# A new front for a hybrid mLSTM / Fourier layer: position products before the modulation, and both modulation halves on TensorE

## What is computed

```python
mod = silu(c) @ w_mod + b_mod
sh1, sc1, g1, sh2, sc2, g2 = split(mod, 6)
h = x * (1 + sc1) + sh1
proj = h @ w_in                       # q, k, v, o, gates, uf, ga, gb
y_b = fourier(uf) @ w_branch_b        # DFT over positions and over the channels of a group
merged = sigmoid(ga) * y_a + sigmoid(gb) * y_b      # y_a: bidirectional mLSTM
x = layer_norm(ALPHA * x + g1 * (merged @ w_out))   # then a SwiGLU FFN, modulated by sh2, sc2, g2
```

## Time and profile before

| | us |
|---|---|
| median of 3 runs (lowest, highest) | 1384.87 (1383.64, 1385.35) |
| span of the profiled execution, first to last instruction | 1382.7 |
| PE busy | 1361.7 |
| VectorE, POOL, ScalarE busy | 860.4, 747.3, 467.1 |
| granted TensorE clock, mean | 0.999 of full |

### The profile page before, as it was taken

How to read it: one execution, slowest core, us unless ns; L and a number is a source line. 1 busy time by engine, 2 the same in 40 slices (tenths; PEclk the granted TensorE clock), 3 DMA queues, 4 the chain that set the end, 5 groups by cost and what they waited for, 6 DMA issues and landing times.

```text
span 1382.7 us, 23138 instructions
## 1 busy us (share of the span) xinstructions
PE 1361.7 (98%) x8693; PEld 1294.0 (94%) x8693; DVE 860.4 (62%) x1458; ACT 467.1 (34%) x828; POOL 747.3 (54%) x417
## 2 busy tenths in 40 slices
PE   9999999999999999999999999989999999999997
PEld 5999999899899989999999999988999999988886
DVE  6875984357426724753587376487877777764307
ACT  4834321231222122221324100266554455463220
POOL 0274775632462354145335666455988889852440
PEclk9999999999999999999999999999999999999999
DMA  9633643211412231142027555613222212242321
GB/s 382 226 108 137 214 149 133 79 64 55 142 68 67 94 109 46 65 145 76 30 91 237 190 183 187 170 64 137 92 91 91 91 62 89 92 168 76 122 77 76
DMA packets 59563, 165.07 MB, mean 119 GB/s; under 512 B 8152, under 2 KB 22624, under 8 KB 58216
## 3 DMA queue, kind: packets, MB, share of 16 engines
q1 hardware_dynamic: 38712, 143.53, 30.3%
q10 hardware_dynamic: 20784, 20.69, 4.7%
HBM read 146.86 MB, written 17.34 MB: 119 GB/s over the span
## 4 chain that ended last, share of the span: by engine, by line
PE 67%; DVE 11%; issue 8%; POOL 6%; DMA 4%; ACT 3%; SPq 0%; DVEq 0%; ACTq 0%; POOLq 0%
PE psum L1425 19%; PE psum L998 15%; PE psum L1462 11%; PE psum L1315 8%; PE psum L1297 3%; PE psum L1063 3%; POOL w_hi L820 3%; POOL w_lo L824 2%; DVE nt_a L2406 2%; PE psum L1169 2%; PE psum L1253 2%; DMA raw<-in_wunits 2%; PE psum L1055 1%; DVE yl L2448 1%; PE psum L1027 1%
## 5 line engine op out<-in xcount | busy, mean ns | idle before, releaser
L820 POOL TENSOR_TENSOR w_hi<-raw,zero 128x1024 fp32r<-128x1024 f32 x78 | 152.3, 1952 | 346.7 <-PE psum L998 280.9
L824 POOL TENSOR_TENSOR w_lo<-raw,w_hi 128x1024 fp32r<-128x1024 f32 (+1 forms) x111 | 268.8, 2422 | 130.6 <-ACT w_hi L2111 73.5
L1425 PE MATMUL psum<-t_r,ws_r 128*128 128x322 f32 x1848 | 276.6, 311 | 2.0 <-POOL ws_r L898 0.7
L1425 PEld LDWEIGHTS psum<-t_r,ws_r 128*128 128x128 f32 x1848 | 275.0, 189 | 3.2 <-issue 2.0
L998 PE MATMUL psum<-h_hi,w_hi 128*128 128x256 f32 (+1 forms) x768 | 176.2, 310 | 1.1 <-PEq L1361 1.0
L998 PE MATMUL psum<-h_lo,w_hi 128*128 128x256 f32 (+1 forms) x768 | 174.9, 309 | 0.0
L998 PE MATMUL psum<-h_hi,w_lo 128*128 128x256 f32 (+1 forms) x768 | 174.8, 309 | 0.0
L898 POOL TENSOR_TENSOR ws_r<-ws_f,ws_r 128x512 fp32r<-128x512 f32 x88 | 124.1, 1410 | 33.7 <-DVE ws_f L2675 20.9
L998 PEld LDWEIGHTS psum<-h_hi,w_hi 128*128 128x128 f32 x768 | 137.8, 188 | 2.4 <-issue 1.7
L998 PEld LDWEIGHTS psum<-h_lo,w_hi 128*128 128x128 f32 x768 | 139.8, 188 | 0.0
L998 PEld LDWEIGHTS psum<-h_hi,w_lo 128*128 128x128 f32 x768 | 139.7, 188 | 0.0
(11 more groups left out here) (359 smaller groups left out, 3070.3 us busy)
## 6 DMA issues: line engine op xcount, KB each, us to landing
raw<-in_wunits SPq DMA_DIRECT2D x124, 512.0 KB, 3.4
pair<-in_wunits SPq DMA_DIRECT2D x46, 512.0 KB, 4.3
mod_slot<-in_wmod SPq DMA_DIRECT2D x16, 512.0 KB, 14.5
mod_ring<-in_wmod ACTq DMA_DIRECT2D x16, 512.0 KB, 3.5
yg_dram<-yg_sb ACTq DMA_DIRECT2D x20, 256.0 KB, 3.0
yg_st<-yg_dram SPq DMA_DIRECT2D x16, 320.0 KB, 3.8
c_raw<-in_stateC SPq DMA_DIRECT2D x4, 1028.0 KB, 6.6
z_ring<-in_wmod SPq DMA_DIRECT2D x8, 512.0 KB, 4.4
```

Of the source, the lines that this page charges most:

```text
L820: pool.tensor_tensor(hi, src, zero[:, 0:1].broadcast_to([P, src.shape[1]]), ALU.add)\
L824: pool.tensor_tensor(lo, src, hi.bitcast(F32), ALU.subtract).then_inc(w_split, 1)
L1425: ins = mm(out, ws_r[n][:, w, cols], t_r[:, n, k, x, :], start=(starts and k == 0 and m == 0), stop=(k == HALF_K - 1 and m == 2), skip_gro ...
```

## The change

- PE's queue: 28 idle products; then all eight odd position tiles, fold by fold over eight banks; the first four scale tiles, three even position tiles, four scale tiles, three even tiles, the transposes, two even tiles; the odd sides of weight 0; all eight shift tiles (first 0, 1, 2, 6, then 7, 3, 4, 5) as two-row products; the odd sides of weight 1 with the shift's transposes after three blocks; the even sides. A modulation part takes the tiles in turn for the first 512 columns, then for the second.
- ScalarE copies position tiles out unscaled in one piece (position_out) and applies the scale when it rounds (position_round, two pieces). VectorE's rest is a two-piece product with a subtraction (e_rest). The zero-position columns go through fix_f, with a rest of their own.
- VectorE loses the sixteen sums of shift_tile, the even sums and the rests of weights 0 and 1; POOL gets the latter two. The bias is added by VectorE (mod_columns).
- SP loads the odd half of the table, the folds, the even half, bmod, eight scale tiles, two weights and five shift tiles; the other three shift tiles follow when the scale parts are done. The table of x, the c rows and weights 2 and 3 follow when the shift parts are done. ScalarE's SiLU of the c rows moves from 22 us to behind h_round(7), ahead of gw_hi.

The diff, cut to its core:

```diff
-POS_BANKS = (4, 5, 6, 7, 2, 3)
+POS_BANKS = (*range(8), 2, 3, 4, 5, 6, 7, 2, 3)
+ROWS_AT = (0, 6)
...
-        N_IDLE = 44
+        N_IDLE = 28
...
-            sp.dma_start(d_st[:], dft_pos).then_inc(table_in, 16)
-            sp.dma_start(bmod_sb[:], bmod).then_inc(bmod_in, 16)
+            sp.dma_start(d_st[:, 1, :, :], dft_pos[:, 1, :, :]).then_inc(table_in, 16)
             for i in range(KT):
                 sp.dma_start(x_rep[:, i, :], x_fold[0, i]).then_inc(xf_in[i], 16)
                 sp.dma_start(x_par[:, i, :], x_fold[1, i]).then_inc(xf_in[i], 16)
...
+            sp.dma_start(d_st[:, 0, :, :], dft_pos[:, 0, :, :]).then_inc(x_in[2], 16)
+            sp.dma_start(bmod_sb[:], bmod).then_inc(bmod_in, 16)
+            scale_in(*range(KD))
             weights(0)
             weights(1)
...
+            for k in (0, 1, 2, 6):
+                shift_in(k)
+            sp.wait_ge(c_sb_in, 16)
+            shift_in(7)
+            sp.wait_ge(mod_done, 2)
+            for k in range(3, 6):
+                sp.wait_ge(shift_landed[k].sem, shift_landed[k].base)
+                shift_in(k)
+            for n in range(3):
                 x_part(n)
...
+            sp.wait_ge(mod_done, 5)
             sp.dma_start(dx_st[:], dft_x).then_inc(table_in, 16)
+            sp.dma_start(silu_z[:], c_rows).then_inc(row_in, 16)
...
+            pool.memset(c_pad[:], 0.0).then_inc(zero_ok, 1)
+            for i in range(KT):
+                pool.wait_ge(fold_ok, i + 1)
+                pool.tensor_tensor(x_rep[:, i, :], x_rep[:, i, :], x_par[:, i, :], ALU.add).then_inc(fold_even_ok, 1)
+            for u in range(2):
+                src, hi, lo = split(u, u, True, n_in=16)
+                pool.wait_ge(w_half, u + 1)
+                rest(src, hi, lo)
...
-            def scale_part(n):
-                pe.wait_ge(mod_in[n], 16)
+            def mod_part(kind, ks, first, last):
+                for k in ks:
+                    if kind == 0:
+                        pe.wait_ge(mod_in[k], 16)
+                    else:
+                        pe.wait_ge(shift_landed[k].sem, shift_landed[k].base + 16)
                 for half in range(2):
-                    ins = mm(psum[0:2, half, :], c_silu[:, n, :], slots[n][:, half * 512:(half + 1) * 512],
-                             start=(n == 0), stop=(n == KD - 1))
+                    for n, k in enumerate(ks):
+                        tile = slots[k if kind == 0 else S_HOME[k]]
+                        ins = mm(psum[0:2, ROWS_AT[kind] + half, :], c_pad[:, k, :],
+                                 tile[:, half * 512:(half + 1) * 512], start=first and n == 0,
+                                 stop=last and n == len(ks) - 1)
                 ins.then_inc(mod_done, 1)
...
+                span = slice(NRC if t else 0, NR)
+                for n, (x, d) in enumerate(((hi, d_hi), (lo, d_hi), (hi, d_lo))):
+                    ins = mm(psum[:, POS_BANKS[i], span], x[:, t, cols], d[:, kind, t, span],
+                             start=(t == 0 and n == 0), stop=(t == KT - 1 and n == 2), skip_group_check=True)
+                return ins
+            def odd_positions():
+                pe.wait_ge(table_ok, 1)
                 for t in range(KT):
...
+                    pe.wait_ge(fold_lo_ok, t + 1)
+                    for i in range(KD):
+                        ins = position_rows(i, t)
+                        if t == KT - 1:
+                            ins.then_inc(pos_done, 1)
+            def even_position(i):
+                if i == KD:
+                    pe.wait_ge(table_ok, 2)
+                    pe.wait_ge(fold_lo_ok, 2 * KT)
+                pe.wait_ge(pos_free, i - 5)
+                for t in range(KT):
+                    ins = position_rows(i, t)
                 ins.then_inc(pos_done, 1)
...
-            for n in range(2):
-                scale_part(n)
-            for i in range(2):
-                position(i)
-            for n in range(2, 6):
-                scale_part(n)
-            position(2)
-            for n in range(6, KD):
-                scale_part(n)
-            position(3)
-            scale_columns()
-            for i in range(4, 2 * KD):
-                position(i)
+            odd_positions()
+            pe.wait_ge(pos_free, 2)
+            mod_part(0, range(4), True, False)
+            for i in range(KD, KD + 3):
+                even_position(i)
+            mod_part(0, range(4, KD), False, True)
+            for i in range(KD + 3, KD + 6):
+                even_position(i)
+            mod_columns(0)
+            for i in range(KD + 6, 2 * KD):
+                even_position(i)
             pe.wait_ge(mod_ready, 1)
-            pe.wait_ge(pos_free, 12)
...
+            pe.wait_ge(w_split, U_PASS1 + 1)
+            for b in range(UB):
+                pe.wait_ge(e_lo_ok, b + 1)
+                side(0, 1, b)
+            pe.wait_ge(pos_free, 2 * KD)
+            mod_part(1, SHIFT_PARTS[0], True, False)
+            mod_part(1, SHIFT_PARTS[1], False, True)
+            pe.wait_ge(w_split, U_PASS1 + 2)
+            for b in range(UB):
+                if b == 3:
+                    mod_columns(1)
+                side(1, 1, b)
+            pe.wait_ge(e_lo_ok, 2 * KD + 1)
             for p in range(2):
                 for b in range(UB):
-                    if p == 0:
-                        pe.wait_ge(e_lo_ok, KD + b + 1)
                     ins = side(p, 0, b)
...
+            def position_out(*tiles):
+                for i in tiles:
+                    kind, f = 1 - i // KD, i % KD
+                    act.wait_ge(pos_done, i + 1)
+                    A_(e_f[:, kind, f, :], psum[:, POS_BANKS[i], 0:NR], ACT.Copy).then_inc(pos_free, 1)
+            def position_round(*tiles):
+                for i in tiles:
+                    kind, f = 1 - i // KD, i % KD
+                    act.wait_ge(pos_free, i + 1)
+                    A_(e_hi[:, kind, f, 0:NRC], e_f[:, kind, f, 0:NRC], ACT.Copy, scale=mod_sb[:, KD + f, 0:1])
+                    A_(e_hi[:, kind, f, NRC:NR], e_f[:, kind, f, NRC:NR], ACT.Copy, scale=mod_sb[:, KD + f, 1:2])\
+                        .then_inc(e_hi_ok, 1)
+            def rows_out(kind):
+                act.wait_ge(mod_done, 3 * kind + 2)
+                for half in range(2):
+                    A_(mod_rows[0:2, kind, half * 512:(half + 1) * 512], psum[0:2, ROWS_AT[kind] + half, :], ACT.Copy)\
+                        .then_inc(sc_rows_ok, 1)
...
+            position_out(*range(KD + 3))
+            rows_out(0)
...
+            position_out(KD + 3)
+            weight_round(0)
+            position_out(KD + 4, KD + 5)
             act.wait_ge(mod_ready, 1)
...
-            weight_round(0)
...
+            position_round(0, 1)
+            position_out(KD + 6)
+            position_round(2)
+            position_out(KD + 7)
+            position_round(3)
             weight_round(1)
...
+            position_round(*range(4, KD + 4))
+            rows_out(1)
+            position_round(*range(KD + 4, 2 * KD))
             act.wait_ge(fix_ok, 1)
-            A_(e_hi[:, 0, :, 0:NRC + 1:NRC], e_f[:, 0, :, 0:NRC + 1:NRC], ACT.Copy).then_inc(e_hi_ok, 1)
+            act.wait_ge(e_lo_ok, 2 * KD)
+            A_(e_hi[:, 0, :, 0:NRC + 1:NRC], fix_f[:], ACT.Copy).then_inc(e_hi_ok, 1)
...
+            act.wait_ge(row_in, 32)
+            for g in range(2):
+                A_(silu_z[:, g, :], silu_z[:, g, :], ACT.Silu).then_inc(row_ok, 1)
...
+            odd_part(2)
+            odd_rest(1)
+            odd_rest(2)
+            d_rest(1, 0)
             v.wait_ge(bmod_in, 16)
             own(plus_one(1))
             plus_one(4).then_inc(bmod_ok, 1)
-            odd_part(2)
-            odd_rest(1)
-            odd_rest(2)
-            for i in range(KT):
-                v.wait_ge(fold_ok, KT)
-                v.tensor_tensor(x_rep[:, i, :], x_rep[:, i, :], x_par[:, i, :], ALU.add).then_inc(fold_ok, 1)
...
+            def e_rest(*tiles):
+                for i in tiles:
+                    kind, f = 1 - i // KD, i % KD
+                    v.wait_ge(e_hi_ok, i + 1)
+                    for g, span in enumerate((slice(0, NRC), slice(NRC, NR))):
+                        ins = v.scalar_tensor_tensor(out=e_lo[:, kind, f, span], in0=e_f[:, kind, f, span],
+                                                     scalar=mod_sb[:, KD + f, g:g + 1],
+                                                     in1=e_hi[:, kind, f, span].bitcast(F32), op0=ALU.mult,
+                                                     op1=ALU.subtract)
+                    ins.then_inc(e_lo_ok, 1)
+            mod_columns(0).then_inc(mod_ready, 1)
+            v.wait_ge(mod_ready, 1)
+            e_rest(*range(KD))
+            v.wait_ge(pos_free, 2 * KD)
+            own(v.tensor_tensor(fix_f[:], e_f[:, 0, :, 0:NRC + 1:NRC], mod_sb[:, KD:2 * KD, :], ALU.mult))
+            e_rest(*range(KD, KD + 4))
+            own(mod_columns(1))
```

(11 more changed lines are left out.)

182 lines of the change are left out of this document (40 added, 142 removed).

## The result

| | before | after |
|---|---|---|
| median of the runs (lowest, highest), us | 1384.87 (1383.64, 1385.35) | 1413.62 (1409.77, 1419.30) |
| the same in a second comparison, us | 1384.67 | 1409.41 (1408.83, 1414.82) |
| span of the profiled execution, us | 1382.7 | 1414.4, and 1407.2 in the second |

The ratio after to before is 1.0212 [1.0195, 1.0230], in the second comparison 1.0186 [1.0158, 1.0215]: slower, by 28.7 and 24.7 us, where 21.9 was forecast. Both intervals lie clear of 1; whether the change costs a full 2% they leave open. In the first comparison the four runs of the changed kernel also spread over 10 us, where those of before spread over 2; in the second it is 6 us (four runs) and 5.5 us (13 runs of before). So the size needs a cause, and so does the wide spread of the first four runs.

What follows compares the result with a forecast made beforehand. PE, busy for 98% of the span, was taken as the bound. 14.6 - 2.8 + 2.7 + 3.8 + 1.2 + 2.4 = 21.9 us on a span of 1382.7 gave 1404.6, as a median 1406.8 us; range 1399 to 1411.

Steps and rivals of the forecast that it cites:

- Work added (+14.6): PE's front: the shift half as two-row products costs 14.0 us and its eight transposes 0.6.
- The start (-2.8): First odd position product: PE starts at 12.6 us against 15.4, 2.8 us earlier.
- the odd waits (+2.7): Odd positions: PE waits 2.1 and 0.5 us for xo_lo of folds 1 and 2, with issue times +2.7.
- The sides (+3.8): First side products: PE waits for VectorE's rests, held up by ScalarE's queue and POOL's rest of weight 1; +3.8 us.
- The closing wait (+1.2): After the shift products: PE waits for the fix's rest before going on; +1.2 us (0 to 2).
- The unit behind (+2.4): Unit that started at 83.25: SiLUs ahead of gw_hi delay POOL's w_lo, a wait of 3 to 4 us; +2.4 (0 to 3).
- if the restart is at +22 and the end isn't: Sign of error: the unit from 83.25 restarts 22 us later, but the run's end isn't later by that.
- rival 2: Start of PE: the clock falls in waits of 1.5 and 2.1 us; +24.4, 1409.3 us; chance 0.09.
- 1 (no blocking): Front: VectorE keeps its pace or the port beside POOL; +16, 1400.9 us; chance 0.15.
- 3 (later waits take it up): Behind 83 us: PE's waits hang on DMA and POOL and hide up to 9 us; 1398 us; chance 0.05.
- 4: Front: two-row modulation products overlap with position products, taking 28.0 us off the path; -6.1, 1378.8 us; chance 0.02.

Runs made afterwards that it cites:

- e_few: Changed kernel with the shift products of six of the eight tiles left out; 1399.3 us, -10.1 to the changed kernel.
- c_12_fix: Changed kernel with column groups, gates' weight, uf and weight 1 roundings reordered, 12 idle products, last four even rests before the fix; 1381.4 us, 0.9982 to before.
- b_two: Kernel before with two useless ScalarE copies ahead of gw_hi, lengthening PE's wait there; 1389.0 us, 1.0031 to before.
- e_even2: Changed kernel with POOL's even sums behind all odd rests and ScalarE's even roundings behind the odd copies; 1407.0 us, -2.4 to the changed kernel.
- e_cols: Changed kernel with the four tiles of a modulation part in four column groups of the array; 1398.5 us, -10.9 to the changed kernel.

## Why the prediction was wrong, step by step

The side was right, the size not: 1406.8 with a range to 1411, and 1413.6 and 1409.4 measured. With the clock alone the time is still inside the range (1409.4); what lies above it goes with the waits for instructions, as far as the one trace of the first comparison shows.

- **Work added (+14.6): right.** 64 two-row records in four groups, 0.435 apart; 13.89 us for 32, and e_few.
- **The start (-2.8) and the odd waits (+2.7): nearly.** PE started at 12.43 (forecast 12.6). VectorE and POOL took turns as read from the earlier trace rows: below, VectorE's xo_lo of one fold takes 2.42, the next two 3.34 each, beside POOL's sums of 2.38 and 3.33. The rests of folds 1 and 2 ended 0.5 and 0.7 earlier than forecast, so PE waited 1.60 instead of 2.1 and hardly at all instead of 0.5, and the sides began at 48.84, forecast 49.6.
- **The sides (+3.8): right wait, wrong price.** The blocker was the one named, POOL's rest of weight 1, and the wait was 2.48. From the first side product to the shift products it took 8.7 us instead of 3.6: 5.1, of which 1.6 is the clock.
- **The closing wait (+1.2): right**, 1.33. c_12_fix, where the same wait (1.76) went with one exchange, shows that it was a matter of order.
- **The unit behind (+2.4): right wait, wrong price.** 3.98 for a forecast 3.7. The chain was the named one (SiLUs 94.76 to 96.7, gw_hi to 97.7, POOL's gw_lo, w_hi, w_lo to 106.3). The clock behind it is another 2.4 us, which no term had.
- **The sum without the clock.** The restart at +23.2, less the 1.6 in the sides, is +21.6, where the sum had +21.9: the start came out 0.8 better than forecast, the other terms a little worse.
- **What was late at the restart, +23.2, is +25.6 at the head loop.** The prediction said it would be wrong "if the restart is at +22 and the end isn't". That is what happened.

Timelines of VectorE and POOL in the profile after, the rows on the turns:

```profile
9.86 2.42 DVE L2161 TENSOR_TENSOR xo_lo<-xo_f,xo_hi 128x1024 fp32r<-128x1024 f32 x1 [1.13 <-ACT xo_hi L1549]
...
14.54 6.68 DVE L2161 TENSOR_TENSOR xo_lo<-xo_f,xo_hi 128x1024 fp32r<-128x1024 f32 x2
```

```profile
8.81 2.38 POOL L826 TENSOR_TENSOR x_rep<-x_rep,x_par 128x1024 f32<-128x1024 f32 x1 [6.59 <-DVE xo_f L2199]
13.49 6.65 POOL L826 TENSOR_TENSOR x_rep<-x_rep,x_par 128x1024 f32<-128x1024 f32 x2 [2.30 <-DVE xo_f L2199]
```

**The step that failed** is rival 2. It had the mechanism, and asked of it only for the waits at the start; there the clock kept its level, behind 1.75 and 1.60. It dismissed it by one row, the 2.3 us wait of the earlier trace rows with the pace kept behind it. But the forecast itself had made a wait of 3.7 us at the restart and one of some 3.3 in the sides (an estimate from its own times: the fifth tile's rest ends near 54.7, and PE is through four blocks at 51.4), both longer than that row, and priced them by their length. The runs showed 2.48 and 3.98, each with a granted clock of 0.50 behind it. With 1.7 to 2.1 by b_two for the wait at the restart and 1.6 in the sides the sum comes to 1410.1 to 1410.5, beside the 1409.4 of the second comparison.

The second cause was not foreseen at all: PE's program grew by 24 records, to a length at which turns of the head loop at times start late, with nine more instruction transfers each. The profile of before showed the loop and the 37 transfers on its page; nothing in it shows where the border is. It makes the first median 4 us higher than the second. That all of these 4 us are this wait isn't shown, since only one execution of the first comparison has a trace; that one lost 5.9 us by it (25.6 to 31.4), 2.82 as a wait and the rest at the low clock.

Of the other rivals: 1 (no blocking) is refuted by VectorE's xo_lo of 2.42 and 3.34 us, and by e_even2. 3 (later waits take it up) happened on a small scale, 1.0 us at the wait for r_all. 4 was rightly given little: as the change has them, the two-row products overlap with nothing. e_cols adds that they do overlap with each other once each has a column group, worth 18.3 us at the restart.

## What to carry over

A wait of TensorE costs its length only as long as the clock stays up behind it: a forecast wait that is longer than any that the profile shows with a full clock gets its length as the lower bound, and a few us at half pace, some 2 us here, on top. When an operand's preparation is moved, look for what else stands in the queue of each engine that prepares it: a few exchanges within the queues of ScalarE and VectorE, and a later start of POOL's even sums, gave 12.8 us here, where all the added work was 14.6. In a program with loops, look at the instruction transfers of two lengths of it before a difference is put down to the edit.
